# Experts in the order of their token counts, weights by register address, and fewer products for small token groups

## The reference

```python
logits = (t @ router_w).astype(jnp.float32)
top_v, top_i = lax.top_k(logits, TOP_K)
gates = jax.nn.softmax(top_v, axis=-1)
combine = jnp.sum(jax.nn.one_hot(top_i, N_EXPERTS, dtype=jnp.float32) * gates[..., None], axis=1)
out = jnp.zeros_like(t)
for e in range(N_EXPERTS):
    out = out + combine[:, e:e + 1].astype(t.dtype) * swiglu(t, w1[e], w3[e], w2[e])
```

## Time and profile before

| | us |
|---|---|
| median of 3 runs (lowest to highest) | 2225.24 (2222.77 to 2225.49) |
| the profiled execution | 2221.32 |
| its span | 2219.5 |
| of it from the first product of expert 0 to the last result of expert 7 | 1141.1 |

### The profile page before, as it was taken

The page is one execution under the profiler, slowest core; times in us unless marked ns, Lnnn a source line. Parts: engine busy times, 40 slices in busy tenths (PEclk is TensorE's granted clock), DMA queues, the critical chain, the costliest instruction groups (busy, mean ns, idle before and its releaser), DMA issues.

```text
span 2219.5 us, 26215 instructions
## 1 busy us (share of the span) xinstructions
PE 2133.1 (96%) x10706; PEld 1726.3 (78%) x10706; DVE 1524.6 (69%) x1811; ACT 1098.8 (50%) x1102; POOL 58.0 (3%) x64
## 2 busy tenths in 40 slices
PE   8989999998898999999999999999999999999998
PEld 7578688884785887878788787888778786758997
DVE  4675644456756888888898886544588888546766
ACT  1232344221321776767677774434367674545554
POOL 0220000002100000000000000000000000100000
PEclk9999999999998999999999999999999999999999
DMA  8202454531023898989899895555579996316460
GB/s 318 76 1 77 181 196 143 201 115 63 1 77 135 304 373 324 372 322 367 327 366 370 323 377 206 184 182 194 185 289 365 327 369 223 114 39 237 163 227 20
DMA packets 209150, 484.44 MB, mean 218 GB/s; under 512 B 9200, under 2 KB 15088, under 8 KB 208112
## 3 DMA queue, kind: packets, MB, share of 16 engines
q1 hardware_dynamic: 209008, 482.50, 60.1%
HBM read 481.44 MB, written 1.05 MB: 217 GB/s over the span
## 4 chain that ended last, share of the span: by engine, by line
PE 84%; DVE 9%; ACT 4%; issue 2%; POOL 1%; DMA 0%; DVEq 0%; ACTq 0%; SPq 0%; POOLq 0%
PE bank L967 20%; PE bank L969 20%; PE bank L968 20%; PE bank L596 11%; PE bank L799 4%; PE bank L603 2%; PE bank L760 1%; DVE e_lo L1844 1%; DVE b_X L1366 1%; ACT e_hi L2249 1%; DVE b_arena L1360 1%; DVE b_XT L1360 1%; DVE b_arena L1366 1%; PE bank L1237 1%; DVE b_arena L1363 1%
## 5 line engine op out<-in xcount | busy, mean ns | idle before, releaser
L1844 DVE TENSOR_TENSOR e_lo<-b_ring,e_hi 128x2048 fp32r<-128x2048 f32 (+1 forms) x407 | 925.0, 2281 | 336.5 <-ACT e_hi L2249 334.0
L2249 ACT ACTIVATE e_hi<-b_ring 128x2048 fp32r<-128x2048 f32 (+1 forms) x407 | 776.7, 1911 | 306.8 <-PE bank L969 302.5
L967 PE MATMUL bank<-e_hi,e_xh 128*128 128x512 f32 (+1 forms) x1200 | 471.8, 393 | 19.7 <-DVE e_lo L1844 10.2
L969 PE MATMUL bank<-e_hi,e_xl 128*128 128x512 f32 (+1 forms) x1200 | 466.0, 388 | 0.0
L968 PE MATMUL bank<-e_lo,e_xh 128*128 128x512 f32 (+1 forms) x1200 | 465.5, 388 | 0.0
L967 PEld LDWEIGHTS bank<-e_hi,e_xh 128*128 128x128 f32 x1200 | 226.6, 189 | 67.4 <-issue 22.0
L967 PE MATMUL bank<-e_hi,e_th 128*128 128x512 f32 x688 | 269.2, 391 | 0.4 <-DVE e_tl L1848 0.4
L968 PE MATMUL bank<-e_lo,e_th 128*128 128x512 f32 x688 | 267.9, 389 | 0.0
L969 PE MATMUL bank<-e_hi,e_tl 128*128 128x512 f32 x688 | 267.7, 389 | 0.0
L969 PEld LDWEIGHTS bank<-e_hi,e_xl 128*128 128x128 f32 x1200 | 226.3, 189 | 47.1
L968 PEld LDWEIGHTS bank<-e_lo,e_xh 128*128 128x128 f32 x1200 | 226.8, 189 | 44.2
(11 more groups left out here) (237 smaller groups left out, 2212.5 us busy)
## 6 DMA issues: line engine op xcount, KB each, us to landing
b_ring<-in_moe_w SPq DMA_DIRECT2D x168, 2048.0 KB, 9.9
b_ring<-in_ffn_w SPq DMA_DIRECT2D x15, 2048.0 KB, 8.3
b_ring<-in_w_in SPq DMA_DIRECT2D x14, 2048.0 KB, 9.7
b_ring<-in_w_up SPq DMA_DIRECT2D x12, 2048.0 KB, 8.0
b_ring<-in_w_down SPq DMA_DIRECT2D x6, 2048.0 KB, 8.7
b_ring<-in_w_o SPq DMA_DIRECT2D x4, 2048.0 KB, 7.9
b_gain<-in_gains SPq DMA_DIRECT2D x6, 1024.0 KB, 4.9
b_ring<-in_w_out SPq DMA_DIRECT2D x2, 2048.0 KB, 7.8
```

The source lines that it names most:

```text
L967: e.matmul(out, ah, bh, start=first, stop=False)
L969: return e.matmul(out, al, bh, start=False, stop=last)
L1844: e.tensor_tensor(lo, raw, r32(hi), ALU.subtract).then_inc(lo_dve.sem)
L2249: return e.activation(out, x, ACT.Copy)
```

## The change

Five things change.

**Order by count.** After the router, DVE ranks the experts by token count. `flag` grows to 16 numbers: 8 to 15 hold which expert takes each of the eight places (given out first, `ids_out`), 0 to 7 whether the place's expert has more tokens than the place's first form holds. Ranks and gates are permuted to places. From here "ex" in the code is a place. For the fixed inputs the places have 138, 121, 79, 49, 43, 39, 38 and 5 tokens.

**Weights by register address.** SP reads the eight numbers into registers and loads each slot from an address computed from them. So no expert load can be issued ahead of the router, and the splits of the first two pieces move behind it.

**16 KB runs.** All large weights are laid out on the host so that a slot is one contiguous 2 MB block, 16 KB for each partition.

**Forms.** A group is "n" (up to 128 tokens, three matmuls) or "a" (up to 64, two matmuls). In "a" the selection matrix holds each token twice, so the stationary operand of 128 columns is the high part of 64 tokens beside the rest part of the same 64 (`e_x[:, z, cc, 64:192]`); it meets the high and then the rest part of the weights (`two`). The two halves of the result are added by one more product with the constant `pairs` (for the gate) and by the turn, which now multiplies with `pairs` (64 columns a chunk). A place has one or two forms in `FORMS`. With these counts places 0 to 7 take "na", "n", "n", "a", "a", "a", "a", "a".

**Gate path in "a".** ACT first copies the w1 result to `e_h` (`g_copy`), PE multiplies it with `pairs` after the first w3 piece (`g_both`), then ACT does Silu.

```diff
+FORMS = [("na", "nn"), ("n", "nn"), ("n", "na")] + [("a", "n")] * 4 + [("a",)]
+ROOM = {"a": 64, "n": 128, "na": 192, "nn": 256}
...
-def rows8(w, lo, n):
-    return w[:, lo:lo + n].rearrange("(c p) n -> p c n", p=128)
+def tile_of(flat_, at, chunks, n):
+
+    return flat_[bass.ds(at, 128 * chunks * n)].rearrange("(p c n) -> p c n", p=128, c=chunks)
...
+        def ranked(r):
+
+            return lambda i, at, chunks, n: lambda ids: tile_of((a["moe_w1"], a["moe_w3"], a["moe_w2"])[i], ids[r] * (D * FFE) + at, chunks, n)
...
+            def two(out, both, bh, bl, first, last):
+                e.matmul(out, both, bh, start=first, stop=False)
+                return e.matmul(out, both, bl, start=False, stop=last)
...
+                            if kinds[s] == "a":
+                                ins = two(b[:, 0:w], e_x[:, z, cc, 64:192], hi[:, w * c:w * c + w], lo[:, w * c:w * c + w], cc == 0, cc == 7)
+                            else:
+                                ins = three(b[:, 0:w], e_xh[z][:, cc, :], e_xl[z][:, cc, :], hi[:, w * c:w * c + w],
+                                            lo[:, w * c:w * c + w], cc == 0, cc == 7)
...
+                    if (kind, hf) == ("w3", 0) and "a" in kinds:
+                        s = kinds.index("a")
+                        e.wait_ge(g_copy.sem, unit - 6 + u + 1)
+                        e.matmul(bank[s][:, 0:w], pairs, e_h[s][:, 0:w], start=True, stop=True).then_inc(g_both.sem)
...
+                                if kinds[s] == "a":
+                                    copy(e_h[s][:, 0:w], bank[s][:, 0:w]).then_inc(g_copy.sem)
+                                else:
+                                    f(e_h[s][:, 0:w], bank[s][:, 0:w], ACT.Silu).then_inc(silu.sem, inc)
...
-                split_rest((FF0_P, MOE_P)[l])
-                split_rest((FF0_P, MOE_P)[l] + 1)
+                if l == 0:
+                    split_rest(FF0_P)
+                    split_rest(FF0_P + 1)
...
-            load(MOE_AT + 2)
+            load(MOE_AT)
             e.wait_ge(*wo_mm(1))
             e.dma_start(rw, a["router_w"][0].rearrange("(c p) n -> p c n", p=128)).then_inc(s_rw, 16)
             load_gain(3, ln_out(2))
+            e.wait_ge(*ids_out(0))
+            ids += nc.values_load_multi_w_load_instructions(flag[0:1, 8:16], [e.engine], min_val=0, max_val=NE - 1,
+                                                            skip_runtime_bounds_check_because="places of eight in order")[1]
             load(IN2_AT + 4)
```

More of the change, by code:

```diff
@@ L59, in constants @@
          "bt0": np.where(b < a, -BIG, 0.0), "bt1": np.where(b > a, -BIG, 0.0),
-         "iota": np.broadcast_to(np.arange(256), (128, 256))}
+         "iota": np.broadcast_to(np.arange(256), (128, 256)), "pairs": a % 64 == b % 64,
+         "most": np.broadcast_to([ROOM[f[0]] + 0.5 for f in FORMS], (128, 8))}
     c["ones"] = np.ones((128, 128))
@@ L484, in use, with gated_uses @@
             uses.append((src, read))
[L486 removed]
+        def gated_uses(tiles_of, widths, first):
             ps = pieces_of(widths)
@@ L1145, in aside @@
                         turn_picks(ex + 1, 0, 2)
-                gated(FFE_UNITS, MOE_P + 42 * ex, unit, tiles, first, aside, [block_of(ex, s) for s in range(2)])
+                gated(FFE_UNITS, MOE_P + 42 * ex, unit, kinds, first, aside, [block_of(ex, s) for s in range(2)])
+                if "a" not in kinds:
+                    e.sem_inc(g_both.sem, 7)
                 if tiles == 2:
@@ L1173, in experts @@
                     with nc.body(f"narrow{ex}", valid_engines=[e.engine]):
-                        expert(ex, 1, wide, hints, [])
-                        e.br(f"done{ex}")
+                        on = []
+                        expert(ex, FORMS[ex][0], wide, hints, on)
+                        end = e.br(f"done{ex}")
+                        for place in on:
+                            end.branch_hint(place)
                     nc.switch_bb(f"done{ex}")
@@ new lines, in router @@
+                ch.wait()
+                ch(e.tensor_reduce(ident_of, picked, AX, ALU.add))
+                ch.wait()
+                e.tensor_copy(flag[:, 8:16], ident_of).then_inc(ids_out.sem)
+                for t in range(2):
+                    ch(tt(ranks[:, t], place_of, bc(rank[:, t, None, :], grid), ALU.mult))
+                ch.wait()
+                ch(e.tensor_reduce(rank[:, :, :], ranks, AX, ALU.add))
+                ch(tt(over, place_of, bc(held[:, None, :], grid), ALU.mult))
@@ new lines, in router @@
+                ch.wait()
+                selected(0, 0)
+                ch(e.tensor_reduce(counts, over, AX, ALU.add))
+                for t in range(2):
+                    ch(tt(shares[:, t], place_of, bc(comb[:, t, None, :], grid), ALU.mult))
+                ch.wait()
+                ch(e.tensor_reduce(comb[:, :, :], shares, AX, ALU.add))
+                ch(tt(e_big[:, :], counts, C("most"), ALU.is_ge))
+                ch.wait()
+                e.tensor_copy(flag[:, 0:8], e_big[:, :]).then_inc(flag_out.sem)
```

241 lines of the change are left out of this document (165 added, 76 removed).

## The result

| | us |
|---|---|
| the changed kernel, median of 4 runs (lowest to highest) | 2152.52 (2145.83 to 2155.81) |
| the kernel before, median of 4 runs beside them | 2224.02 (2222.77 to 2225.49) |
| ratio, 95% interval | 0.9677 (0.9662 to 0.9692) |
| predicted | 2137, range 2111 to 2177 |
| the profiled execution; its span | 2155.81; 2153.9 |

The kernel became 3.2% faster. The forecast was 15.5 us low, inside the range.

What follows compares the result with a forecast made beforehand. PE bounds the kernel before, DVE places 3 to 7 after. 734 + 204.3 + 134.8 + 126.4 + 4 x 115 + 111 = 1770.5 us ends the experts, 88.3 less: 2133.0 profiled, plus 3.9, 2137, range 2111 to 2177.

Steps and rivals of the forecast that it cites:

- The start: Ahead of place 0: expert numbers out at 709 us, first product at 733 where it was 717.67.
- elsewhere: 0: Outside the steps counted for start and experts: long runs help only where PE waits for a load, so 0 us.
- Place 0: Two-group expert from its first product: 241.2 - 38.1 + 3.1 - 1.9 = 204.3 us.
- seven products with `pairs`, 3.1 us: In place 0 and each "a" place: seven added fp32 products of 512 columns, 0.44 us each, 3.1 us.
- Places 1 and 2: The two "n" places stay as before, since PE bounds them: 134.8 and 126.4 us.
- Places 3 to 6: "a" places, DVE the bound: 107.6 us of its work plus 3.5 and 3.5 of waits, 115 us each.
- The 3.5 for the chain through `pairs`: In an "a" place: ACT late once a unit, DVE waiting 0.4 to 0.6 us, seven times, 3.5 us.
- The other 3.5, for the change of expert: Between "a" places: DVE waits 1.5 us for `e_xh` and some 2 to read the flag and branch.
- Transfers as the bound: Rival: DMA engines bound the five "a" places, 121 us each, 2167 us in all, or 2177 at 123; chance 0.15.
- Easy handoffs: Rival: DVE hardly waits, 110 us per "a" place, 2112 us, or 2110 with a shorter start; chance 0.12.
- The clock: Rival: PE's clock falls to its lower level, some 165 us per "a" place, 2387 us in all; chance 0.03.
- The order costing more than it brings: Rival: forms not taken, or order costs more than it brings; "n" from place 1 on, 2194 us; chance 0.01.

Runs made afterwards that it cites:

- number 1: The change with three products for every group in all places, keeping order by count, register addresses and long runs, against the kernel before: 2230.73 us, ratio 1.0031.
- number 2: The change with only place 0 put back to three matmuls for both groups: 2178.93 us, ratio 0.9805 to the kernel before.
- number 3: The kernel before with only the 16 KB layout of all large weights added: 2225.21 us, ratio 1.0008.
- Number 8: The change without the gate's product with `pairs` and the copy ahead of it, Silu reading the bank directly: 2131.51 us, ratio 0.9581 to the kernel before.
- number 5: The change with the Silu of "a" forms issued one step later, behind ACT's rounding of the next piece: 2135.3 us, ratio 0.9595 to the kernel before.
- numbers 4 and 10: The change with expert weights in 2 and 4 KB runs: 2149.46 us; change with late Silu and early selection, half the bytes in places 3 to 7: 2130.38 us.
- number 9: The change with late Silu and early selection, DVE computing only half of each rest in places 3 to 7: 2089.99 us, ratio 0.9407 to the kernel before.

## Why the prediction came out as it did

Right: the forms as counted, PE no longer the bound, DVE in its place, PE's clock at 0.98 to 1.00 in the "a" places, the transfers hidden. Of its signs, two came out a little weaker: DVE is busy 91.5% of an "a" place (107.0 of 116.95) and not over 93%, and the share of 0.94 to 0.96 belongs to 376 GB/s and not to 383. By its own steps:

- **The start.** The first product came at 738.2 in this profile where 733 to 734 was forecast, but at 734.2 and 733.5 in the profiles of numbers 1 and 2, which do the same up to there. From the expert numbers on the chain was right: 22.8 us from the CAST to the first product, for the 24 from 709 to 733. The CAST itself came at 715.4, 6.4 us after the forecast's 709. This lies in a part that the prediction called "elsewhere: 0": in the profile of the change the run of fp32 products of the earlier trace rows stands 8.6 us later, well ahead of anything that the experts do:

```profile
10.94 13.31 PE L613 MATMUL bank<-b_XT,b_ring 128*128 128x256 f32 x48 [2.29 <-DMA b_ring<-in_w_in]
...
693.43 6.17 PE L633 MATMUL bank<-b_cst 128*128 128x512 f32 x14
```

  In the twelve experiments it stands at 687.4 to 691.3, in number 3, the layout alone, at 687.4. So a few microseconds are lost early in every profile with the long runs, between 2.5 and 8.6 against the one profile of the kernel before. In the profile of the change PE waits 2.29 us for the first weights, and TensorE's granted clock is 0.76 from 80 to 90 us, where the kernel before has 1.00. Number 3's time doesn't show a loss, and the cause stays open.
- **Place 0**: 211.0 us against 204.3 and 1 for the clock. The term "seven products with `pairs`, 3.1 us" was half of what it is: it took the 14 records of the earlier trace rows for 14 products. Number 8 gives 6.3, which is 3.2 more. The turn's second record a chunk was left out altogether. The turn of both groups, read to the start of the next product, took 0.79 us in the kernel before (first two lines) and takes 1.25 in the change (the others), 0.46 more and seven times:

```profile
1389.86 1.03 PE L603 MATMUL bank<-b_cst,e_h 128*128 128x128 f32 x8
1390.65 0.48 PE L967 MATMUL bank<-e_hi,e_xh 128*128 128x512 f32 x1
```

```profile
761.90 0.60 PE L620 MATMUL bank<-b_cst,e_h 128*128 128x128 f32 x4
762.34 1.00 PE L1008 MATMUL bank<-b_cst,e_h 128*128 128x64 f32 x8
763.15 0.48 PE L984 MATMUL bank<-e_hi,e_x 128*128 128x512 f32 x1
```

  204.3 + 3.2 + 3.2 = 210.7, so the two account for the place, and the 1 us for the clock was not needed. They also close number 2: 38.1 - 6.3 - 3.2 = 28.6, for the 28.4 measured.
- **Places 1 and 2**: 133.6 and 128.1 against 134.8 and 126.4, 0.5 us more together.
- **Places 3 to 6**: 117 against 115. DVE's busy time was right (107.0 against 107.6). The 3.5 for the chain through `pairs` was right in mechanism and about in size: number 5 took it out, and the place fell by 3.9 (the mean of four from 116.9 to 113.0). The other 3.5, for the change of expert, came out at 2.1: its 2 us for DVE's flag and branch were taken from a bubble of PE, and DVE has no such gap. The term that failed is one that wasn't there. "In each unit ACT is late once" was wrong: it is late a second time, where the rounding stands behind the wait for the turn, 0.6 us in most units and 4.3 in a place. Number 5, without the wait behind `pairs`, still has these 4.3 in its 6.3 us of waits for `e_hi`. Four places and the last (112.9 against 111) make 9.5 us of the error.
- **The sum.** The profiled execution took 2155.8 us, where the forecast's sum gives 2133.0 for one: 22.8 low. That is 5.2 from the start, 5.7 from place 0, 0.5 from places 1 and 2, 9.5 from the "a" places and 1.8 behind the experts. That the forecast of the median is no more than 15.5 low is luck: it added 3.9 us, since the profiled execution before was that much under the median, and the one after was 3.3 above it.
- **The rivals.** Transfers as the bound: refuted by numbers 4 and 10. Easy handoffs at 110 us a place: even number 5 has 113. The clock: it stayed. The order costing more than it brings: by itself it does, as far as number 1 shows, where order, addresses and long runs together cost some 6 us (the runs alone, by number 3, nothing that the measurement tells). With the forms it pays; no run tries the forms without the order, so what the order is worth to them is not shown.
- The limit of some 358 GB/s on the memory's side, by the Trainium skill, "DMA: Bandwidth & Descriptors", section "Where 436 GB/s comes from", does not show on this one core: 376 over a place in the change, 414 in number 9.

## What to carry to other kernels

When the bounding engine is relieved, the waits of the next one come out of hiding. They are found by writing down, for each input of that engine, what stands ahead of it in its producer's queue: here two instructions of ACT that wait for PE, each ahead of a rounding that its place in the queue held back. Moving one of them by a step brought 18 us, nearly as much as leaving out the work that it waited for (21 us, 6.3 of them in place 0, where PE is the bound); the other was not moved. Before a duration is taken from a run of equal records, count the records against the instructions in the code; and a rate of transfers seen under a busy engine is a demand, not a limit.

## What the runs showed of the hardware

- A product of 512 columns in plain fp32 leaves two records and takes some 0.9 us of PE; one of 64 columns also leaves two, and four of them take 0.81 us to the start of the next product.
- One core loaded at 414 GB/s over 106 us, at a DMA share of 0.99, in runs of 16 KB; runs of 2 and 4 KB carried 378 at a share of 1.01.
- DVE and GpSimd, both subtracting one SBUF tile from another, hold each other out: 0.73 us for GpSimd's part alone, 2.57 beside a DVE instruction that began just ahead of it; DVE's part took 2.03 us when it began first and 2.27 on average.
